# Values with a column of ones as the moving side: mLSTM outputs by tokens in a one-core diffusion step

## The reference, cut to what matters

```
num = inter[..., None] * einsum('bhtd,bhdv->bhtv', qc, c_prev) + einsum('bhts,bhsv->bhtv', s, vc)
den = inter * einsum('bhtd,bhd->bht', qc, n_prev) + sum(s, axis=-1)
h = num / maximum(abs(den), exp(-m_t))[..., None]
...
h_ml = h_f + rev(h_b)
y_ml = head_rms(h_ml, ml_out_g) * sigmoid(mo)
```

## Time and profile before

| | |
|---|---|
| median of 3 runs | 3552.4 us |
| profiled execution | 3546.18 us, of it span 3544.4 us |
| PE busy | 3176.0 us (90%), 17384 records |
| DVE, ACT, POOL busy | 1965.2, 1318.5, 600.3 us |
| values projected in layer 0 and layer 1, end | 195.35 and 1984.12 us |
| output gate (`U_MO`) starts, layer 0 and layer 1 | 331.15 and 2121.05 us |

### The profile page before, as it was taken

One profiled execution on the slowest core, in us unless ns is written; L12 is line 12 of the kernel. 1 busy time (PEld: TensorE's weight loads), 2 busy tenths in 40 slices (PEclk: granted clock), 3 DMA queues, 4 the chain that ended last, 5 costly groups with the idle time before them and its releaser, 6 DMA issues.

```text
span 3544.4 us, 42018 instructions
## 1 busy us (share of the span) xinstructions
PE 3176.0 (90%) x17384; PEld 2464.9 (70%) x17384; DVE 1965.2 (55%) x2100; ACT 1318.5 (37%) x1654; POOL 600.3 (17%) x250
## 2 busy tenths in 40 slices
PE   4989968999997799999978799789998769999998
PEld 3855957877777567667648649669887756667665
DVE  2446653201222798888974474633014259898887
ACT  2123322001002576766752133220000137676775
POOL 2410342322121100000013203423223110000000
PEclk8979979999997899999989799789999979999999
DMA  8510441365560498988985304512333129898987
GB/s 209 70 33 7 66 100 42 96 150 159 176 187 24 167 351 295 335 299 309 325 239 72 42 0 66 88 40 58 72 68 73 69 92 348 291 349 288 342 300 252
DMA packets 350925, 580.26 MB, mean 164 GB/s; under 512 B 13648, under 2 KB 140624, under 8 KB 350480
## 3 DMA queue, kind: packets, MB, share of 16 engines
q1 hardware_dynamic: 297488, 501.26, 48.5%
q10 hardware_dynamic: 42784, 45.58, 3.9%
q0 software_dynamic: 10464, 30.74, 2.8%
HBM read 568.08 MB, written 9.45 MB: 163 GB/s over the span
## 4 chain that ended last, share of the span: by engine, by line
PE 72%; DVE 8%; DMA 7%; issue 4%; ACT 4%; DVEq 3%; POOL 1%; POOLq 0%; ACTq 0%; SPq 0%
PE ps L766 25%; PE ps L1169 8%; PE ps L1172 8%; PE ps L1177 8%; PE ps L737 6%; DMA ring<-w_down 2%; DMA arena<-ada_w 2%; PE ps L1086 2%; PE ps L794 2%; DVEq L1697 1%; PE ps L818 1%; PE ps L981 1%; PE ps L857 1%; PE ps L869 1%; PE ps L1050 1%
## 5 line engine op out<-in xcount | busy, mean ns | idle before, releaser
L766 PE MATMUL ps<-h_hi,w_hi 128*128 128x320 f32 x1856 | 587.8, 317 | 72.7 <-DVE h_lo L2000 45.7
L1930 DVE TENSOR_TENSOR w_lo<-ring,w_hi 128x2048 fp32r<-128x2048 f32 x256 | 583.6, 2287 | 106.2 <-ACT w_hi L1296 105.9
L766 PE MATMUL ps<-h_lo,w_hi 128*128 128x320 f32 x1856 | 575.8, 310 | 0.0
L766 PE MATMUL ps<-h_hi,w_lo 128*128 128x320 f32 x1856 | 575.8, 310 | 0.0
L1296 ACT ACTIVATE w_hi<-ring 128x2048 fp32r<-128x2048 f32 x256 | 486.5, 1910 | 86.8 <-DMA ring<-w_up 27.2
L766 PEld LDWEIGHTS ps<-h_hi,w_hi 128*128 128x128 f32 x1856 | 350.4, 189 | 94.6 <-issue 74.6
L1349 ACT ACTIVATE arena<-ps,par 128x640 f32<-128x640 f32 x88 | 69.9, 794 | 821.8 <-PE ps L766 821.7
L610 POOL TENSOR_TENSOR w_lo<-ring,w_hi 128x2048 fp32r<-128x2048 f32 (+1 forms) x76 | 348.1, 4581 | 30.3 <-issue 30.3
L766 PEld LDWEIGHTS ps<-h_lo,w_hi 128*128 128x128 f32 x1856 | 350.9, 189 | 2.1 <-issue 0.5
L766 PEld LDWEIGHTS ps<-h_hi,w_lo 128*128 128x128 f32 x1856 | 350.6, 189 | 0.0
L608 POOL CAST w_hi<-ring 128x2048 fp32r<-128x2048 f32 (+1 forms) x76 | 143.5, 1888 | 1016.0 <-PEq L754 636.5
(11 more groups left out here) (264 smaller groups left out, 5285.3 us busy)
## 6 DMA issues: line engine op xcount, KB each, us to landing
ring<-w_gate SPq DMA_DIRECT2D x128, 1024.0 KB, 6.0
ring<-w_up SPq DMA_DIRECT2D x128, 1024.0 KB, 6.1
ring<-w_down SPq DMA_DIRECT2D x128, 1024.0 KB, 6.7
ring<-w_in SPq DMA_DIRECT2D x64, 1024.0 KB, 11.9
arena<-ada_w ACTq DMA_DIRECT2D x40, 1024.0 KB, 5.3
ring<-ada_w SPq DMA_DIRECT2D x8, 1024.0 KB, 11.8
arena<-biasT POOLq DMA_DIRECT2D x16, 512.0 KB, 4.5
ring<-w_o SPq DMA_DIRECT2D x8, 1024.0 KB, 12.7
```

The costliest lines, as they stand in the source:

```text
L766: last = pe.matmul(ps[:, bank(u) + half, 0:HALF], w[:, k, f0:f0 + P], a[:, k, at], start=(k == 0 and part == 0), stop=(k == KD - 1 and par ...
L1930: dve.tensor_tensor(w_los[g % NW], ring[:, s, :], w_his[g % NW].bitcast(F32), ALU.subtract).then_inc(slot_used[s], 1)
```

## The change

- The latent sums are turned round. The score weights of 128 keys by 128 queries, and the scaled queries `qi`, now stay in the array, and the values move, with a column of ones behind each head's 128 values (`mvx`, 129 columns). `c0x` is the given state with the normaliser as its 129th column. One matmul gives numerator and denominator, with tokens on partitions: a step has 14 matmuls of 129 columns, into banks 6 and 7.
- The second broadcast (`rowM`) is gone. Its values per token are turned into columns once, with the gate columns, and ACT takes exp(-m) of all of them at once (`emcol`). The matrix `emm` goes.
- `copy_nums` copies both banks into `nums`. `combine` handles both directions of a head together: maxima and reciprocals on 128 by 8 elements, one product on 128 by 8 by 128, and one sum into `h_ml` (tokens by head dimension).
- The context steps of all heads run together (`context`, `context_sums`): 8 exponent rows at once, one exponential per head and direction. The final states come after the last latent step, as eight matmuls in a row with three copies.
- Broadcasts for the two directions have a bank each (4 and 5), and score blocks signal one by one.
- The head norm sums squares on ACT along the free side (`squares`, with `accum_out`), and takes one root and one reciprocal of 128 by 20. `turn_heads` turns the scaled `h_ml` back by 20 transposes in the place of `head_sums`, and `heads_out` multiplies by gain and output gate out of PSUM.

```diff
...
-mv = view(5120, NTILE, WB)
...
+mvx = view(5120, NTILE, HM, VX)
...
+c0x = view(W_AT + 5120, 8, VX)
+nums = [view(ROWS_AT + 4 * T, 8, VX), view(W_AT + 5120 + 8 * VX, 8, VX)]
...
+h_ml = view(Y_TOP, HM, NTILE, P)
...
+steps = [(hd, d) for hd in range(HM) for d in range(2)]
...
+def turn_heads(l):
+    for hd in range(HM):
+        pe.wait_ge(*h_scaled.at(l, hd + 1))
+        free_unit(l, U_TURN + hd)
+        b = bank(U_TURN + hd)
+        for t in range(NTILE):
+            last = pe.transpose(ps[:, b + t // 4, t % 4 * P:(t % 4 + 1) * P], h_ml[:, hd, t, :], ident)
+        last.then_inc(unit_full.sem, 1)
...
+def context():
+    for hd in range(HM):
+        last = pe.matmul(ps[:, 0, hd * P:(hd + 1) * P], mk[:, hd, 0:TP], mq[:, hd, 0:TP],
+                         start=True, stop=True)
+    last.then_inc(ctx_st_ready.sem, 1)
+    for d in range(2):
+        for hd in range(HM):
+            last = pe.matmul(ps[:, 1 + d, hd * P:(hd + 1) * P], pick(d, hd), rowB[0:8, d, 0:TP],
+                             start=True, stop=True)
+        last.then_inc(ctx_bc_ready.sem, 1)
+    for hd in range(HM):
+        last = pe.transpose(ps[:, 3, hd * P:(hd + 1) * P], mk[:, hd, 0:TP], ident)
+    last.then_inc(ktok_ps.sem, 1)
+def context_sums():
+    pe.wait_ge(*ctx_w_ready.at(l, 2))
+    for c in range(8):
+        d, hd = c // HM, c % HM
+        b, at = triple(c)
+        if c == 6:
+            pe.wait_ge(*ktok_ready.at(l, 1))
+        last = pe.matmul(ps[:, (6, 7, 3)[b], at], wctx[:, d, hd, :], mvx[:, 0, hd, :],
+                         start=True, stop=True)
+    last.then_inc(ctx_nd_ready.sem, 1)
...
+def broadcast(s):
+    hd, d = steps[s]
+    if s >= 2:
+        pe.wait_ge(*e_ready.at(l, 4 * (s - 1)))
+    pe.matmul(ps[:, 4 + d, :], pick(d, hd), rowB[0:8, d, TP:T], start=True, stop=True)\
         .then_inc(bc_ready.sem, 1)
+def scores(hd):
+    if hd:
+        pe.wait_ge(*w_ready.at(l, 8 * hd))
+    else:
+        pe.wait_ge(*wend_sum.at(l, 1))
+    for i in range(4):
+        if hd == 0 and i == 3:
+            pe.wait_ge(*ctx_copied.at(l, 1))
+        at = TP + i * P
+        pe.matmul(ps[:, i, :], mk[:, hd, at:at + P], mq[:, hd, TP:T], start=True, stop=True)\
+            .then_inc(st_ready.sem, 1)
...
 def sums(s):
...
+    hd, d = steps[s]
     if s:
         pe.wait_ge(*num_copied.at(l, s))
...
+    pe.wait_ge(*qi_ready.at(l, s + 1))
+    for n in range(4):
+        j = n if d == 0 else 3 - n
+        pe.wait_ge(*w_ready.at(l, 4 * s + n + 1))
+        out = ps[:, 6 + j // 2, j % 2 * VX:(j % 2 + 1) * VX]
+        at = slice(j * P, (j + 1) * P)
+        pe.matmul(out, qi[:, s % 2, at], c0x[:, d * HM + hd, :], start=True, stop=False)
+        keys = list(range(j + 1)) if d == 0 else list(range(3, j - 1, -1))
+        for i in keys:
+            last = pe.matmul(out, wmat[:, s % 2, i, at], mvx[:, 1 + i, hd, :],
+                             start=False, stop=(i == keys[-1]))
     last.then_inc(nd_ready.sem, 1)
...
+context()
+broadcast(0)
+broadcast(1)
+context_sums()
+for hd in range(HM):
+    scores(hd)
+    if hd:
+        sums(2 * hd - 1)
+    if hd < HM - 1:
+        broadcast(2 * hd + 2)
+    sums(2 * hd)
+    if hd < HM - 1:
+        broadcast(2 * hd + 3)
+sums(2 * HM - 1)
+final_states()
...
+def context():
+    for d in range(2):
+        act.wait_ge(*ctx_z_ready.at(l, d + 1))
+        for hd in range(HM):
+            last = act.activation(wctx[:, d, hd, :], wctx[:, d, hd, :], ACT.Exp,
+                                  bias=acol[:, d, 0, d * HM + hd:d * HM + hd + 1])
+        last.then_inc(ctx_e_ready.sem, 1)
+    act.wait_ge(*wend_sum.at(l, 1))
+    act.activation(wend[:, :], wend[:, :], ACT.Exp).then_inc(wend_ready.sem, 1)
+    act.wait_ge(*ktok_ps.at(l, 1))
+    act.activation(ktok, ps[:, 3, :].rearrange("p (a b) -> p a b", a=HM), ACT.Copy,
+                   scale=ML_SCALE).then_inc(ktok_ready.sem, 1)
...
+def copy_nums(s):
+    hd, d = steps[s]
+    act.wait_ge(*nd_ready.at(l, s + 1))
+    if hd:
+        act.wait_ge(*h_done.at(l, hd))
+    act.activation(nums[hd % 2][:, 4 * d:4 * d + 4, :].rearrange("p (a b) c -> p a (b c)", a=2),
+                   ps[:, 6:8, 0:2 * VX], ACT.Copy).then_inc(num_copied.sem, 1)
...
+context()
+exponentials(0)
+act.wait_ge(*ctx_nd_ready.at(l, 1))
+copy_triples(nums[1], (6, 7, 3)).then_inc(ctx_copied.sem, 1)
+exponentials(1)
+act.wait_ge(*state_out.at(l, 2))
+for s in range(2 * HM):
+    copy_nums(s)
+    if s + 2 < 2 * HM:
+        exponentials(s + 2)
+    if s in (2, 4, 6):
+        squares((None, 0, 1)[s // 2 - 1])
+act.wait_ge(*state_ps.at(l, 1))
+copy_triples(cout, (2, 3, 4)).then_inc(state_copied.sem, 1)
+squares(2)
+squares(3)
+act.activation(hss, hss, ACT.Sqrt, bias=eps[:, :], scale=1.0 / P).then_inc(h_root.sem, 1)
...
+def combine(hd):
+    if hd is None:
+        dve.wait_ge(*ctx_copied.at(l, 1))
+        n8, out = nums[1], h_ml[:, :, 0, :]
+    else:
+        dve.wait_ge(*num_copied.at(l, 2 * hd + 2))
+        n8, out = nums[hd % 2], h_ml[:, hd, 1:NTILE, :]
+    for d in range(2):
+        em = emcol[:, d, 0, d * HM:(d + 1) * HM] if hd is None else emcol[:, d, 1:NTILE, d * HM + hd]
+        den = n8[:, 4 * d:4 * d + 4, P]
+        dve.scalar_tensor_tensor(recip8[:, 4 * d:4 * d + 4], den, -1.0, em, ALU.mult, ALU.max)
     dve.drain()
...
+    for d in range(2):
+        den = n8[:, 4 * d:4 * d + 4, P]
+        dve.tensor_tensor(recip8[:, 4 * d:4 * d + 4], den, recip8[:, 4 * d:4 * d + 4], ALU.max)
     dve.drain()
...
+    dve.reciprocal(recip8, recip8)
     dve.drain()
...
+    dve.tensor_tensor(n8[:, :, 0:P], n8[:, :, 0:P], recip8[:, :, None].to_broadcast([P, 8, P]), ALU.mult)
+    dve.drain()
+    dve.tensor_tensor(out, n8[:, 0:4, 0:P], n8[:, 4:8, 0:P], ALU.add).then_inc(h_done.sem, 1)
+context()
+exponents(0)
+exponents(1)
+context_weights()
+for hd in range(HM):
+    weights(2 * hd)
+    if hd:
+        exponents(2 * hd + 1)
+    weights(2 * hd + 1)
+    if hd < HM - 1:
+        exponents(2 * hd + 2)
     else:
...
+        state_values()
+    combine(hd - 1 if hd else None)
+combine(HM - 1)
+dve.wait_ge(*h_root.at(l, 1))
+dve.reciprocal(hss, hss)
+dve.drain()
+for hd in range(HM):
+    dve.tensor_tensor(h_ml[:, hd, :, :], h_ml[:, hd, :, :],
+                      hss[:, hd, :][:, :, None].to_broadcast([P, NTILE, P]), ALU.mult)\
+        .then_inc(h_scaled.sem, 1)
...
+def heads_out(l):
+    for hd in range(HM):
+        u = U_TURN + hd
+        dve.wait_ge(*emptied(l, U_MO + hd))
+        dve.wait_ge(*filled(l, u))
+        for b, lo, hi in ((0, 0, 512), (1, 512, T)):
+            last = dve.scalar_tensor_tensor(y_ml[:, hd, lo:hi], ps[:, bank(u) + b, 0:hi - lo],
+                                            par[:, Q_OG + hd:Q_OG + hd + 1], sig_mo[:, hd, lo:hi],
+                                            ALU.mult, ALU.mult)
+        last.then_inc(dve_emptied.sem, 1)
+        dve.drain()
+        dve.sem_inc(yml_ready.sem, 1)
...
+act.activation(acol[:, :, :, :].rearrange("p a b c -> p (a b c)"), ps[:, 0, 0:80], ACT.Copy)
+act.activation(emcol[:, :, :, :].rearrange("p a b c -> p (a b c)"), ps[:, 0, 80:160], ACT.Exp,
+               scale=-1.0).then_inc(acol_ready.sem, 1)
...```

PE, layer 0, one latent step as it stands before (the second broadcast, then the sums; tiles named as above; the scores of the head stand ahead of it):

```order
L880 MATMUL ps<-arena,cst 128x512
L881 MATMUL ps<-arena,cst 128x512
L895 MATMUL ps<-arena 128x512
L897 MATMUL ps<-arena,cst 128x512
L895 MATMUL ps<-arena 128x384
L897 MATMUL ps<-arena,cst 128x384
L895 MATMUL ps<-arena 128x256
L897 MATMUL ps<-arena,cst 128x256
L895 MATMUL ps<-arena 128x128
L897 MATMUL ps<-arena,cst 128x128
L900 MATMUL ps<-arena 128x512
L901 MATMUL ps<-arena,par 128x512
```

More of the change, by code:

```diff
@@ L167, in step_program @@
         acol = sb("acol", [P, 2, NTILE, 8])
+        emcol = sb("emcol", [P, 2, NTILE, 8])
         wr = sb("wr", [P, KD, NE])
@@ L492, in step_program, with stiles @@
         SEG = [(0, TP), (TP, T)]
[L494 to L502, removed]
+        steps = [(hd, d) for hd in range(HM) for d in range(2)]
+        def stiles(d):
             if d == 0:
@@ L861, in mlstm @@
             def mlstm(l):
-                def scores(s):
-                    g, hd, d = steps[s]
-                    n = g * HM + hd
-                    if s:
-                        pe.wait_ge(*w_ready.at(l, e_before[s]))
-                    lo, hi = SEG[g]
-                    for i in range((hi - lo) // P):
-                        last = pe.matmul(ps[:, i, 0:hi - lo], mk[:, hd, lo + i * P:lo + (i + 1) * P],
-                                         mq[:, hd, lo:hi], start=True, stop=True)
-                    last.then_inc(st_ready.sem, 1)
@@ L920, in final_states @@
-                    pe.wait_ge(*state_copied.at(l, 8))
-                for s in range(16):
-                    if s == 8:
-                        sums(7)
-                        final_states()
-                    if steps[s][2] == 0:
-                        scores(s)
```

(36 more changed lines are left out.)

318 lines of the change are left out of this document (120 added, 198 removed).

## The result

The changed kernel takes 3414.7 us (median of 4 runs, 3412.82 to 3416.32), beside 3552.93 for the kernel before, run with it (median of 4): a ratio of 0.9608, interval 0.9592 to 0.9625. The forecast was 3408, its range 3394 to 3440. The profiled execution takes 3412.82 us, its span 3411.0 (the earlier trace rows for before: 3544.4).

What follows compares the result with a forecast made beforehand. PE nearly filled the head period and DVE's inversion closed it. Savings of 70.5 + 71.7 + 2 x (2.3 - 1.3) = 144.2 us took the profiled 3546.2 to 3402.0, a median of 3408; range 3394 to 3440.

Steps and rivals of the forecast that it cites:

- What bounds: Latent heads before: PE nearly fills the 21.3 us period, DVE's inversion closes it; both have to fall.
- The price of 0.22 per narrow matmul: Latent and context sums: a matmul of 129 moving columns takes 0.22 us at full clock.
- Rivals 2 and 4: 2: weight loads not hidden, 0.43 per narrow matmul, 3462, chance 0.08; 4: narrow sums eat the gain, 3570, chance 0.015.
- the estimate by the Trainium skill: Narrow matmuls: 0.32 us each at 129 columns, making the layer's 128 of them 13 us more.
- The period: Latent heads after: 11.4 us of chain beside 11.3 of PE work, plus 0.3, a period of 11.7.
- the slack that I had added: Latent head period: 0.3 us added for hand-offs that the walk misses.
- My sum of PE's work before: Latent head before the change: PE work of 18.9 us, with 2.4 of waiting.
- The context: Layer 0, values' projection to context sums: PE work 9.5 us at partly half clock, sums 1.8, done at 213.0.
- The last head: End of the latent part: scores, sums, exponentials, weights' tail and eight final-state matmuls, 15.9 us in all.
- Together: Stage from values' projection to gate projection: 65.3 us in each layer, 70.5 and 71.7 less than before.
- the table load: Before the query norm: square root table loaded again, 1.28 us per layer taken in full, bounds 0 and 1.3.
- Rivals 1, 3 and 5: 1: other engines close the period, 3422 or 3434, 0.14; 3: clock stays half, 3506, 0.05; 5: wait behind stage, 0.015.

Runs made afterwards that it cites:

- e1: The kernel before without the reciprocal of the inverted denominators, outputs left undivided: 3534.2 us, ratio 0.9949.
- e5: The changed kernel with each of the latents' sums moving 65 of its 129 columns: 3455.3 us, ratio 0.9725.
- e4: The changed kernel with one dead 128x1 square root on ACT behind the output gate's sigmoids, loading its table early: 3405.0 us, ratio 0.9583.
- e2: The changed kernel with two dead 128x448 reciprocals on DVE behind each head's combination: 3435.2 us, ratio 0.9664.
- e3: The changed kernel with four dummy 512-column matmuls per layer filling PE's waits in the context: 3400.9 us, ratio 0.9573.
- e12: The changed kernel with context broadcasts moved earlier, plus three dummy 512-column matmuls per layer among the narrow ones: 3408.6 us, ratio 0.9599.

## Why the prediction was right

- **What bounds.** PE's work and DVE's inversion nearly tied, as forecast, and both had to fall: taking the inversion away alone gave 1.6 us per period (e1), and with the inversion left in, DVE's 17.41 per period would have held it (an estimate from the earlier trace rows).
- **The price of 0.22 per narrow matmul** held: 0.22 on the chain after, and e5 shows that at 129 columns it stands just where the weight load alone would also put it. Rivals 2 and 4 fall with it: load and columns are not added. The surcharge that the Trainium skill's "TensorE: Matmul & The Clock Gate", section "Back-to-back issue gap", gives for streams of loads and matmuls does not show in float32 at this width. The chain after has 0.22 a matmul, where the estimate by the Trainium skill was 0.32.
- **The period** came out at 12.18, not 11.7, and for another reason than walked: I had the chain through DVE and ACT at 11.4 and PE at 11.3, and PE alone takes 12.18. The term that was too small is the broadcast: 1.05, not 0.86, and another 0.2 on the work behind it (a first pair of the sums 0.42 instead of 0.22, scores 3.63 instead of 3.43), twice per head: some 0.8 more of PE work, 0.5 beyond the slack that I had added. That is 1.0 in two heads and 0.6 in the first. The trace of before had these prices:

```profile
282.99 1.05 PE ps L880 x2
284.04 0.86 PE ps L881 x2
284.90 1.06 PE ps L895 x2
```

The first broadcast of a pair and the matmul behind the pair cost 0.2 more than the 0.86 that I took. My sum of PE's work before, 18.9, was short by the same 0.8: the earlier trace rows have PE busy for 19.97 us in a period, and e1, with PE busy all of the time, has 19.7.
- **The context** was 2.6 us too short, mostly in one term: I let the context's sums run at full clock (1.8), and they took 3.60 at 0.55. In layer 1 the clock stayed at half into the first scores as well (4.34). The start of the sums, 15.9 us behind the values, was 16.6. Half clock in the rest, taken from the earlier trace rows, was right, though PE took 10.5 there and not 9.5.
- **The last head** came out at 16.7 instead of 15.9: two of ACT's copies (0.61 each) stand alone on the chain, since banks 6 and 7 are all that the sums have.
- **Together** the stages are 70.2 and 70.8 instead of 65.3, 10.4 us: this is the miss. Behind the stage it was the other way: `turn_heads` saved 2.2 per layer as forecast, but the table load, which I charged with 1.3 per layer, is absorbed (e4), 2.6 in all: the lower of the two bounds that I gave it. Some 3 us were lost elsewhere: behind the stage of layer 1 the kernel before takes 1423.4 us and the kernel after 1423.6, so that nothing of the 2.2 shows there, in a stretch that scatters by more.
- **The median.** The profiled execution missed by 3412.8 - 3402.0 = 10.8, the median by 6.7, because the profiled execution of after lies 1.9 below its median and that of before 6.2. That the median came so near is in this part luck.
- **Rivals 1, 3 and 5** did not come. The first was close, 2.2 us of DVE per head away (e2); a clock that falls within the heads, as in the third, is what the kernel with 65 columns got (e5). The gate projection follows the final states at once, so there is no wait for the fifth.

## What to carry to other kernels

Turning a product round so that narrow values move paid here with 129 moving columns, which take about as long as a weight load; at 65 nothing more was saved, and the clock fell on top. When two engines nearly tie, price both alone: here the spectacular operation, a reciprocal of 3.35 us per step, gave by itself a sixth of what the period gained, yet without taking it away PE's cut could not have paid in full. Check a price list against the kernel before: a sum that comes out below the engine's busy time there lacks a price. And an operation that is added to a path with a later stall costs only what it exceeds that stall by, so look down the chain for the next wait before charging it.

## What the runs showed of the hardware that I had not expected

- The granted clock fell within work of PE that had no pause: within the heads of e5 (0.70 on average, where 129 columns in place of 65 kept 1.00), in the first wide broadcast of e3 at about 204.4 us, without a pause since 195.67, and in e12 at about 203.0, without a pause since 198.99. What decides it in the context these runs do not settle; e3 shows that it can be at full there for some 4 us (200.2 to 204.4), and e5 only that it was lower with 65 columns than with 129.
- A 512-column matmul whose weights have 8 rows, behind matmuls with 128, took 0.19 us more than others of its width (1.05 instead of 0.86), and the first one with 128 rows behind it 0.20 more (0.42 instead of 0.22); of two with 8 rows in a row only the first did (1.05, then 0.86, in the kernel before).
